# Clock-holding products, full-row broadcasts and a new order between the input projection and RWKV, in a two-layer hybrid SSD / RWKV-7 / mLSTM step on one Trainium2 core

## The chip, the cores and the metric

The kernel runs on one core of a Trainium2 chip. The metric is the device time of one execution in microseconds (us); lower is better. The engines are TensorE (PE; PEld is its weight load), VectorE (DVE), ScalarE (ACT), GpSimd (POOL) and SyncE (SP), which issues the transfers. The two levels of TensorE's clock that occur here are 1.2 and 2.4 GHz; the profile prints the granted clock as 0.50 and 1.00 (a stretch with both has a value between).

## The reference, cut to what matters

Two trunk layers work on 128 context tokens and 512 latent tokens, 640 in all, model width 1024. Float32 throughout.

```python
h = _rms_norm(x, norm1_g) * (1 + sc1) + sh1
u = h @ w_in                                   # one projection for three mixers
y_ssd  = ssd_mixer(...)      # Mamba-2, 8 heads of 64, chunks of 128, forward and backward, summed
y_rwkv = rwkv_mixer(...)     # RWKV-7, 4 heads of 64, forward and backward, summed
y_ml   = mlstm_mixer(...)    # 4 heads of 64, chunks of 128, forward and backward, summed
x = x + g1 * (concat(y_ssd, y_rwkv, y_ml) @ w_out)
x = x + g2 * ((silu(h2 @ ffn_w1) * (h2 @ ffn_w3)) @ ffn_w2)
```

In a chunk of the SSD scan, with t and s tokens of the chunk:

```python
decay  = exp(acum[t] - acum[s])  where s <= t, else 0
scores = einsum(C[t], B[s]) * decay
y      = einsum(scores, x * dt) + einsum(C[t], state_at_start) * exp(acum[t])
state' = state * exp(acum[last]) + einsum(exp(acum[last] - acum[s]), B, x * dt)
```

The mLSTM has the same form with its own gates (`wts`, `num`, `den`), and its output is `num / max(|den|, exp(-m))`. RWKV needs per token the decay, the rate `lr`, and the keys `kd = k * (1 + (lr - 1) * k_a)`; its two directions run as chunks of 128 with a small triangular inverse.

## The kernel before, in words

All 640 tokens stand as five chunks (NC = 5): chunk 0 is the context, 1 to 4 the latent tokens. Features lie on partitions, tokens along the free dimension. The body is written out for each of the two layers (`lay`), and each engine has its own hand-written program; semaphores (`s[...]`) tie them. The order of an engine's work is the order in which its program is written.

Of a layer, this is the part between the input projection and the RWKV scan, TensorE's side first:

1. After the last block of `w_in` (`mm3`, L878 to L880, three products of 320 columns for a float32-like result) come eight pairs of small products with the LoRA weights, 32 contraction rows each (L944, four rounds of four instructions). Each round waits until ACT has read the banks of the round before (`pair_read`, ACT at L1583).
2. The cached states are turned (L955, L959, L960), and the decays between chunks are spread over the partitions (L970, L972). ACT copies both out (L1674 to L1681). `token_major(c)` (L988 to L994) turns a chunk's features to tokens on partitions, ACT copies them (L1703 to L1707), DVE makes `XEB` from them (L2120, L2124) and POOL `VEB` (L685, `end_values`). `chunk_states(c)` (L1008 to L1031) multiplies these with the keys. TensorE runs `token_major(c + 1)` before `chunk_states(c)`.
3. The loop over chunks for y. `w_rows(c, i)`, i = 0 to 5, is a pair: one product that copies a row of log decays over all partitions (L1057; a selection column broadcast, 60 contraction rows, 512 columns) and one that adds the mask `NEG` of large negative numbers (L1058, bfloat16). ACT takes the exponential (L1719), four instructions a pair. `qk_products(c)` (L1113, L1117) gives the scores, DVE multiplies both (`weights`, L2143), and `y_ssd(c, g)` (L1089, and L1103 with the states for c > 0) and `y_mlstm(c)` (L1128, and L1140 with the states) use the result. `e_rows(c)` (L1072, 12 contraction rows) spreads the decays by which DVE scales the queries (`scaled_queries`). `mlstm_back(c)` (L1152) turns the mLSTM's result back after DVE's `normalise` (L2176 to L2184). Row products use banks 2, 3 and 5 in turn and wait until the bank has been read.
4. RWKV. POOL makes scaled keys (`chunk_keys`, L732 to L739), TensorE turns them (L1196, L1198) and makes diagonal blocks (L1207, L1212), DVE masks them (L2252 to L2263), then the inverse begins (L1221) and products with 256 columns follow (L1239).

DVE's side: `keys(c)`, in the loop of stage 2, works out what RWKV needs of its keys for all tokens (L2098, two instructions of 640 columns for c = 0 and 2; L2103 and L2104, 1280 columns each, for c = 1 and 3). POOL's side: after `end_values(c)` it scales the skip path of x (L688), then makes scaled values (`scaled_values`, L698) and combines states (`start_state`, L647 to L657); in RWKV it runs `chunk_keys(0)`, then `gates()` (L665 to L675, six passes over 640 to 2560 columns: the SSD gate and RWKV's bonus term), then `chunk_levels(k)` (L750) and `chunk_keys(k + 1)`. What `gates()` makes is read after the last RWKV chunk.

SELr has zeros in rows 60 to 127. RX is the left half of the buffer `whi`; its first 60 rows arrive by DMA.

## Time and profile before

| | |
|---|---|
| time, 3 runs | 2513.01 us median, 2505.12 to 2514.81 |
| the profiled execution | 2509.3 us, of which the span is 2507.6 us |
| busy, share of the span | PE 89%, PEld 82%, DVE 33%, ACT 30%, POOL 29% |
| mean granted clock of TensorE | 0.907 |
| chain that ended last, by engine | PE 80%, DVE 9%, ACT 4%, issue 3%, DMA 2%, POOL 2% |

The three projections' products (L878, L879, L880) hold 55% of the chain. They run at granted clock 1.00 for nearly all of their time. The part that the change touches stands between 292 and 480 us in layer 0 and between 1516 and 1700 us in layer 1. In the page's row of the granted clock, by fortieths of the span, these are the two places with the lowest digits (6, 5, 6 and 6, 5).

### The profile page before, as it was taken

How to read it: one execution, taken by the hardware profiler on the slowest of the kernel's cores; microseconds unless marked ns; L12 is line 12 of the kernel's file. 1: busy time of each engine (PE TensorE's matmuls, PEld its weight loads, DVE VectorE, ACT ScalarE, POOL GpSimd, SP SyncE). 2: the span in 40 equal slices, each digit the busy share in tenths (PEclk: the TensorE clock that was granted, in tenths of full speed). 3: DMA queues.
4: the chain of work that ended last, by engine and by line, in shares of the span. 5: the costliest groups of instructions: out<-in, count | busy, mean ns of one | idle time of the engine just before them, and what ended most of it. 6: DMA issues, size and time to landing. Idle time of an engine off the chain costs nothing.

```text
span 2507.6 us, 45740 instructions
## 1 busy us (share of the span) xinstructions
PE 2234.2 (89%) x20426; PEld 2044.9 (82%) x20426; DVE 821.7 (33%) x1363; ACT 762.1 (30%) x1348; POOL 723.0 (29%) x539
## 2 busy tenths in 40 slices
PE   5899899788797999999978998988887799999996
PEld 4899766677597999999878986657776799999986
DVE  4655153555512101010046453345544300101003
ACT  3435342232323222221153453323332422222111
POOL 4233150422022333332212322324221133333321
PEclk8999856799898999999989997659998999999998
DMA  6444200100021222243325431010001122222221
GB/s 222 136 142 126 58 7 1 35 5 3 1 60 51 76 76 76 76 123 114 85 82 156 142 105 19 1 34 5 3 2 33 42 78 73 73 75 74 70 61 57
DMA packets 260496, 166.66 MB, mean 66 GB/s; under 512 B 29938, under 2 KB 234228, under 8 KB 260300
## 3 DMA queue, kind: packets, MB, share of 16 engines
q1 hardware_dynamic: 259846, 163.59, 22.3%
q8 instruction: 161, 2.64, 0.4%
q14 instruction: 35, 0.29, 0.0%
q10 hardware_dynamic: 454, 0.14, 0.0%
HBM read 159.59 MB, written 4.12 MB: 65 GB/s over the span
## 4 chain that ended last, share of the span: by engine, by line
PE 80%; DVE 9%; ACT 4%; issue 3%; DMA 2%; POOL 2%; SPq 0%; DVEq 0%; ACTq 0%; POOLq 0%
PE PS L878 19%; PE PS L880 18%; PE PS L879 18%; PE PS L1221 4%; PE PS L829 2%; DMA ring<-in_w_in 2%; PE PS L1057 1%; PE PS L1089 1%; POOL ring_r L791 1%; PE PS L842 1%; PE PS L1058 1%; PE PS L1128 1%; DVE arena L1879 1%; PE PS L1103 1%; PE PS L1239 1%
## 5 line engine op out<-in xcount | busy, mean ns | idle before, releaser
L878 PE MATMUL PS<-rwp_r,whi_r 128*128 128x320 f32 x2880 | 912.6, 317 | 75.6 <-DVE arena_r L1883 35.9
L880 PE MATMUL PS<-rwp_r,ring_r 128*128 128x320 f32 x2880 | 901.4, 313 | 0.0
L791 POOL TENSOR_TENSOR ring_r<-ring,whi_r 128x1024 fp32r<-128x1024 f32 (+1 forms) x204 | 493.7, 2422 | 1254.4 <-ACT whi_r L1554 1254.4
L879 PE MATMUL PS<-arena_r,whi_r 128*128 128x320 f32 x2240 | 700.5, 313 | 0.0
L878 PEld LDWEIGHTS PS<-rwp_r,whi_r 128*128 128x128 f32 x2880 | 552.2, 192 | 93.4 <-issue 48.9
L880 PEld LDWEIGHTS PS<-rwp_r,ring_r 128*128 128x128 f32 x2880 | 551.4, 191 | 0.0
L879 PEld LDWEIGHTS PS<-arena_r,whi_r 128*128 128x128 f32 x2240 | 428.6, 191 | 0.0
L1554 ACT ACTIVATE whi_r<-ring 128x1024 fp32r<-128x1024 f32 (+1 forms) x204 | 211.5, 1039 | 678.6 <-PE PS L880 599.8
L879 PE MATMUL PS<-U_r,whi_r 128*128 128x320 f32 x960 | 300.3, 313 | 0.0
L2410 DVE TENSOR_TENSOR U<-arena,PS 128x640 f32<-128x640 f32 x44 | 36.1, 821 | 557.6 <-PE PS L880 557.6
L879 PEld LDWEIGHTS PS<-U_r,whi_r 128*128 128x128 f32 x960 | 183.8, 191 | 1.9 <-issue 0.2
L1221 PE MATMUL PS<-arena 64*64 64x64 f32 x3840 | 140.6, 226 | 49.1 <-DVE arena L2261 29.4
L2389 DVE SCALAR_TENSOR_TENSOR x<-PS,MOD,x 128x128 f32<-128x128 f32 (+2 forms) x96 | 36.1, 434 | 435.1 <-PE PS L880 435.1
L1221 PEld LDWEIGHTS PS<-arena 64*64 64x64 f32 x3840 | 127.7, 140 | 62.0 <-DVE arena L2261 32.3
L1820 ACT ACTIVATE arena<-PS 128x640 f32<-128x640 f32 x44 | 31.0, 705 | 271.5 <-PE PS L880 271.5
L1719 ACT ACTIVATE arena<-PS,arena 128x128 f32<-128x128 f32 x240 | 68.1, 373 | 129.5 <-PE PS L1058 125.4
L1751 ACT ACTIVATE arena<-PS 128x512 f32<-128x512 f32 (+1 forms) x100 | 55.5, 555 | 148.7 <-PE PS L1221 133.0
L1583 ACT ACTIVATE U<-PS 128x640 f32<-128x640 f32 x56 | 39.2, 699 | 152.8 <-PE PS L880 152.5
L1941 DVE SCALAR_TENSOR_TENSOR arena<-U,PC,arena 128x127 f32<-128x127 f32 x80 | 63.8, 817 | 51.9 <-ACT arena L1595 50.2
L750 POOL TENSOR_TENSOR arena<-arena,MKC 128x256 f32<-128x256 f32 x40 | 34.9, 893 | 138.6 <-DVE arena L2256 138.6
L829 PE MATMUL PS<-arena,ones 128*128 128x320 f32 x160 | 50.3, 450 | 22.4 <-ACT arena L1510 22.4
L732 POOL TENSOR_TENSOR arena<-rwp,U 128x256 f32<-128x256 f32 x20 | 14.6, 729 | 184.0 <-DVE U L2148 113.0
(364 smaller groups left out, 2793.9 us busy)
## 6 DMA issues: line engine op xcount, KB each, us to landing
ring<-in_ffn_w SPq DMA_DIRECT2D x120, 512.0 KB, 3.8
rwp<-in_ada_w SPq DMA_DIRECT2D x64, 512.0 KB, 4.1
ring<-in_w_in SPq DMA_DIRECT2D x50, 512.0 KB, 5.6
U<-in_ada_w SPq DMA_DIRECT2D x16, 512.0 KB, 10.1
ring<-in_w_out SPq DMA_DIRECT2D x16, 512.0 KB, 4.3
arena<-in_ada_w SPq DMA_DIRECT2D x16, 512.0 KB, 4.7
ring<-in_ffn_w SPq DMA_DIRECT2D x16, 384.0 KB, 3.4
out<-U SPq DMA_DIRECT2D x5, 512.0 KB, 2.7
```

The costliest lines, as they stand in the source:

```text
L791: g.tensor_tensor(rings_r[:, slot_of[n], 0:size(n), :], slot(n)[:, 0:size(n), :], whis[:, q_ % 2, 0:size(n), :].bitcast(F32), ALU.subtract ...
L829: ins = mm(PS[:, hf, 0:HALF], ones[:, :], tmp[:, k % 2, hf * HALF:(hf + 1) * HALF], start=k == 0, stop=k == KT - 1)
L878: mm(out, w[0][:, k, :], hi[:, cols], start=start, stop=False)
L879: mm(out, w[0][:, k, :], lo[:, cols], start=False, stop=False)
L880: return mm(out, w[1][:, k, :], hi[:, cols], start=False, stop=stop)
L1221: ins = mm(PS[t_, 4 * d + bank, col0 + 64 * hh:col0 + 64 * hh + 64], b[lhs][t_, hh, :], IDC[t_, :] if rhs is None else b[rhs][t_, hh, :], ...
L1554: A(whis[:, q % 2, 0:size(n), :], slot(n)[:, 0:size(n), :], ACT.Copy).then_inc(s["split_hi"], 1)
L1583: A(out.rearrange("p (a t) -> p a t", a=2), PS[:, b:b + 2, 0:HALF], func, **kw).then_inc(s["pair_read"], 1)
L1719: ins = A(W[:, i, q * P:(q + 1) * P], PS[:, ROW_BANK[(9 * c + i) % 3], q * P:(q + 1) * P], ACT.Exp, bias=COLS[:, c, 1, r + q:r + q + 1])
L1751: A(b["QQ"][:, w], PS[:, a + 2, :].rearrange("p (w h t) -> p w h t", w=2, h=4)[:, w], ACT.Copy).then_inc(s["inv_copy"], 1)
L1941: return v.scalar_tensor_tensor(out=out, in0=in_, scalar=s, in1=out, op0=ALU.mult, op1=ALU.add)
L2389: ins = v.scalar_tensor_tensor(out=xv[:, m, t0:t1], in0=PS[:, bank, c0:c0 + t1 - t0], scalar=g[:, cond:cond + 1], in1=xv[:, m, t0:t1], op0 ...
```

## The change

- A helper `warm(n, b)` issues n products of 128 rows and 512 columns (bfloat16 identity times `NEG`) into bank b. Nothing reads them. They stand: four ahead of the LoRA rounds and three behind each of the four rounds (bank 0), two ahead of each `chunk_states` wait (bank 4), eight ahead of the first wait for RWKV's keys and eight ahead of the first wait for its features (bank 7). That is 42 a layer.
- `w_rows` uses all 128 contraction rows instead of 60. `e_rows` becomes a pair: behind each of the three products one more of 128 rows adds a column of `NEG` that is all zero, 12 more products of 512 columns a layer.
- The turning of the states and the spreading of the decays move behind `token_major(0)`; ACT's copies of them move likewise (`states_in`). `qk_products(0)` moves ahead of the last `chunk_states`.
- In the loop, `mlstm_back(c - 1)` moves ahead of `y_ssd(c, 0)`; `y_mlstm` is cut in two, and the first three `w_rows` of the next chunk are spread around its second half and `qk_products`.
- DVE: `keys` has one instruction a chunk in stage 2; the three last passes move into the loop (`keys_end`, chunks 0 to 2, behind `weights`). POOL: the skip scaling leaves `end_values` and follows later; `gates()` moves from behind `chunk_keys(0)` to the end of RWKV.

```diff
@@ -702,11 +705,13 @@
                     def scans():
 ...
                         for c in range(NC):
                             end_values(c)
                         scaled_values(0)
+                        skip(0)
 ...
                         for k in range(1, 4):
                             start_state(k, 0)
+                        skip(1)
                         for c in range(2, NC):
                             scaled_values(c)
+                            skip(c)
@@ -754,11 +761,11 @@
                         chunk_keys(0)
-                        gates()
                         for k in range(NC):
                             chunk_levels(k)
                             if k < NC - 1:
                                 chunk_keys(k + 1)
+                        gates()
@@ -933,8 +940,15 @@
+                    def warm(n, b):
+
+                        for _ in range(n):
+                            mm(PS[:, b, :], identb[:, :], NEG[:, :].unsqueeze(1).broadcast_to((P, 2, 2 * P)),
+                               start=True, stop=True)
+
                     pe.wait_ge(s["lora_in"], at["lora_in"] + 48)
+                    warm(4, 0)
                     for i in range(0, len(LORAS), 2):
 ...
+                        warm(3, 0)
@@ -1001,6 +1019,7 @@
                         dirs = [d for d in range(2) if (c < 4 if d == 0 else c > 1)]
+                        warm(2, 4)
                         pe.wait_ge(s["xe_ready"], at["xe_ready"] + c + 1)
@@ -1033,10 +1052,25 @@
                     token_major(0)
+                    states_turned()
                     for c in range(NC):
                         if c < NC - 1:
                             token_major(c + 1)
+                        else:
+                            pe.wait_ge(s["ta_act"], at["ta_act"] + 4 * NC)
+                            qk_products(0)
                         chunk_states(c)
@@ -1054,7 +1088,7 @@
-                        mm(PS[:, b, :], SELr[0:NX, r:r + 1].broadcast_to((NX, P)), RX[0:NX, :], start=True, stop=False)
+                        mm(PS[:, b, :], SELr[:, r:r + 1].broadcast_to((P, P)), RX, start=True, stop=False)
@@ -1069,8 +1103,10 @@
-                            mm(PS[:, b, :], SELEr[e, i * P:(i + 1) * P], EX[e, :], start=True, stop=True).then_inc(
-                                s["ec_mm"], 1)
+
+                            mm(PS[:, b, :], SELEr[e, i * P:(i + 1) * P], EX[e, :], start=True, stop=False)
+                            mm(PS[:, b, :], identb[:, :], NEG[:, P - 1:P].broadcast_to((P, 4 * P)), start=False,
+                               stop=True).then_inc(s["ec_mm"], 1)
@@ -1153,27 +1183,28 @@
                         w_rows(c, 3)
+                        if c:
+                            mlstm_back(c - 1)
                         y_ssd(c, 0)
                         for i in range(4, 6):
                             w_rows(c, i)
                         y_ssd(c, 1)
-                        if c:
-                            mlstm_back(c - 1)
                         if c < NC - 1:
                             e_rows(c + 1)
                         y_mlstm(c)
                         if c < NC - 1:
+                            w_rows(c + 1, 0)
+                        y_mlstm_state(c)
+                        if c < NC - 1:
+                            w_rows(c + 1, 1)
                             qk_products(c + 1)
-                            for i in range(3):
-                                w_rows(c + 1, i)
+                            w_rows(c + 1, 2)
@@ -1185,6 +1216,8 @@
+                            if i == 0:
+                                warm(8, 7)
                             pe.wait_ge(s["rw_keys"], at["rw_keys"] + i + 1)
@@ -1200,6 +1233,8 @@
+                            if i == 0:
+                                warm(8, 7)
                             pe.wait_ge(s["rw_feat"], at["rw_feat"] + i + 1)
@@ -1705,8 +1743,10 @@
                         A(BKB[c % 2], PS[:, bk_, 0:384], ACT.Copy).then_inc(s["ta_act"], 1)
-                        if c > 0:
+                        if c:
                             chunk_states(c - 1)
+                        else:
+                            states_in()
@@ -2092,19 +2132,26 @@
-                        d = c // 2
-                        if c % 2 == 0:
-                            for f in range(2):
-                                ins = v.tensor_scalar(KD[d][:, f, :], BB[d][:, f, :], col(lay, "rwkv_k_a", f),
-                                                      KAO[:, f:f + 1], ALU.mult, ALU.add)
-                            ins.then_inc(s["dve_step"], 1)
+                        if c == 4:
+                            v.tensor_tensor(KD[0], KD[0], U[:, RK_:RK_ + 2, :], ALU.mult).then_inc(s["dve_step"], 1)
+                        else:
+                            d, f = c // 2, c % 2
+                            v.tensor_scalar(KD[d][:, f, :], BB[d][:, f, :], col(lay, "rwkv_k_a", f),
+                                            KAO[:, f:f + 1], ALU.mult, ALU.add).then_inc(s["dve_step"], 1)
+                        dve.wait_ge(s["dve_step"], step())
+
+                    def keys_end(c):
+
+                        if c == 0:
+                            v.tensor_tensor(KD[1], KD[1], U[:, RK_:RK_ + 2, :], ALU.mult).then_inc(s["dve_step"], 1)
+                        else:
+                            d = c - 1
+                            v.tensor_tensor(BB[d], BB[d], KK, ALU.mult).then_inc(
+                                s["rw_ready"] if d else s["dve_step"], 1)
 ...
@@ -2220,6 +2266,8 @@
                         for i in range(4, 6):
                             weights(c, i)
+                        if c < 3:
+                            keys_end(c)
                         y_back(c)
```

TensorE, from the LoRA rounds (L944, after: L958) to the states (L955, after: L976) and the first chunk (L988, after: L1006), before:

```order
L944 MATMUL PS<-arena,lora 128x320 x16
L955 MATMUL PS<-ident,arena 64x64 x8
...
L988 MATMUL PS<-ident,U 128x128 x4
L990 MATMUL PS<-ident,U 128x128 x2
L992 MATMUL PS<-ident,arena 128x24 x5
L994 MATMUL PS<-ident,U 128x128 x3
```

and now, where L946 is `warm`:

```order
L946 MATMUL PS<-NEG,identb 128x512 x4
L958 MATMUL PS<-arena,lora 128x320 x4
L946 MATMUL PS<-NEG,identb 128x512 x3
...
L1006 MATMUL PS<-ident,U 128x128 x4
L1008 MATMUL PS<-ident,U 128x128 x2
L1010 MATMUL PS<-ident,arena 128x24 x5
L1012 MATMUL PS<-ident,U 128x128 x3
L976 MATMUL PS<-ident,arena 64x64 x8
```

The first chunk's turning has passed the states, and unread products stand in each round.

TensorE, end of chunk 1 of the loop, before (L1072 is `e_rows`, L1128 and L1140 `y_mlstm`, L1113 and L1117 `qk_products`, L1057 and L1058 `w_rows`):

```order
L1152 MATMUL PS<-ident,arena 128x128 x4
L1072 MATMUL PS<-whi_r,SELE 128x512 x3
L1128 MATMUL PS<-ring,arena 128x65 x8
L1140 MATMUL PS<-arena 128x65 x8
L1113 MATMUL PS<-U 128x128 x2
L1117 MATMUL PS<-U 128x128 x4
L1057 MATMUL PS<-whi_r,SEL 128x512
L1058 MATMUL PS<-NEG,identb 128x512
```

and at the end of chunk 0 now (same roles: L1107 and L1108, L1153, L1058 and L1062, L1091 and L1092; chunk 0 has no part with states, in the others it stands between the first two pairs of L1091):

```order
L1107 MATMUL PS<-whi_r,SELE 128x512
L1108 MATMUL PS<-NEG,identb 128x512
L1153 MATMUL PS<-ring,arena 128x65 x8
L1091 MATMUL PS<-whi_r,SEL 128x512
L1092 MATMUL PS<-NEG,identb 128x512
...
L1058 MATMUL PS<-U 128x128 x2
L1062 MATMUL PS<-U 128x128 x4
...
L1182 MATMUL PS<-ident,arena 128x128 x4
L1125 MATMUL PS<-arena,whi 64x128 x8
```

Products of 512 columns now stand on both sides of each narrow part, and the turning back (L1182) has moved behind them.

POOL at the start of RWKV, before:

```order
L739 TENSOR_TENSOR arena<-U 128x2x128
L665 TENSOR_TENSOR U<-U 128x2560
L670 TENSOR_TENSOR U<-rwp 128x1280
L672 TENSOR_TENSOR U<-U 128x1280
L675 TENSOR_SCALAR U<-U,PC 128x640 x2
L750 TENSOR_TENSOR arena<-arena,MKC 128x256 x4
```

and now:

```order
L746 TENSOR_TENSOR arena<-U 128x2x128
L757 TENSOR_TENSOR arena<-arena,MKC 128x256 x4
```

The four lines of `gates()` are gone from here; they stand behind the fifth L757.

## Rows read from the trace of the kernel before

**Rows 1.** Windows view: stretch, us, busy PE, PEld, DVE, ACT, POOL, clock, DMA.

```profile
292.93:308.28 15.35, 8.85 (x32) 4.56 (x33) 0.08 (x1) 7.07 (x9) 0.00 (x0) 0.58 0.20 34
308.28:346.04 37.76, 33.20 (x257) 27.39 (x258) 22.66 (x23) 13.46 (x44) 18.56 (x17) 0.59 0.10 12
346.04:457.07 111.03, 104.72 (x596) 71.00 (x594) 41.40 (x83) 36.84 (x129) 22.18 (x33) 0.61 0.00 1
457.07:476.96 19.89, 8.84 (x140) 7.65 (x140) 13.17 (x12) 2.34 (x5) 19.10 (x12) 0.50 0.40 106
1516.61:1530.92 14.31, 7.85 (x32) 4.07 (x33) 0.08 (x1) 7.07 (x9) 0.00 (x0) 0.64 0.22 37
1530.92:1566.90 35.98, 31.16 (x259) 25.80 (x259) 22.66 (x23) 13.54 (x44) 18.26 (x17) 0.64 0.08 12
1566.90:1678.97 112.07, 106.44 (x596) 71.14 (x594) 41.41 (x83) 37.10 (x129) 22.09 (x33) 0.59 0.00 1
```

**Rows 2.** The same columns, two slices of the loop over chunks.

```profile
370.00:372.50 2.50, 2.50 (x18) 1.73 (x16) 0.00 (x0) 0.00 (x0) 0.00 (x0) 0.50 0.00 0
397.50:400.00 2.50, 2.50 (x33) 2.04 (x29) 0.00 (x0) 0.88 (x4) 0.95 (x1) 1.00 0.00 0
```

**Rows 3.** Timeline, TensorE, at granted clock 0.50: start us, us, engine, line, operation.

```profile
356.39 1.65 PE L1072 MATMUL PS<-whi_r,SELE 12*128 12x512 f32 x3
357.96 3.68 PE L1128 MATMUL PS<-ring,arena 128*128 128x65 f32 x16
...
362.16 1.06 PE L1117 MATMUL PS<-U 64*128 64x128 f32 x8
...
372.97 0.79 PE L1057 MATMUL PS<-whi_r,SEL 60*128 60x512 f32 x1
...
374.23 1.98 PE L1089 MATMUL PS<-arena,whi 128*64 128x128 f32 x16
```

**Rows 4.** Timeline, TensorE, at granted clock 1.00.

```profile
396.09 0.50 PE L1057 MATMUL PS<-whi_r,SEL 60*128 60x512 f32 x1
...
396.52 0.39 PE L1058 MATMUL PS<-NEG,identb 128*128 128x512 bf16 x1
...
396.84 1.09 PE L1089 MATMUL PS<-arena 128*64 128x128 f32 x16
...
449.49 2.00 PE L1128 MATMUL PS<-ring,arena 128*128 128x65 f32 x16 [1.71 <-DVE arena L2143]
...
451.42 1.77 PE L1140 MATMUL PS<-arena,lora 64*128 64x65 f32 x16
```

**Rows 5.** Timeline, TensorE: three waits outside the loop (in brackets, us and releaser).

```profile
295.90 2.50 PE L944 MATMUL PS<-arena,lora 32*128 32x320 f32 x8 [1.62 <-ACT rwp L1583]
...
343.32 1.12 PE L1025 MATMUL PS<-arena 128*64 128x256 f32 x4 [4.02 <-DVE arena L2124]
...
459.16 1.08 PE L1196 MATMUL PS<-ident,arena 128*128 128x128 f32 x4 [2.10 <-POOL arena L733]
```

**Rows 6.** Waits, 308.28 to 477 us: who waited for whom, total us, times, longest.

```profile
PE PS L1128 <- DVE arena L2143: 3.4, 3, 1.7
```

**Rows 7.** Groups by line, DVE, 292.93 to 476.96 us: busy us, mean ns.

```profile
L2261 DVE TENSOR_TENSOR arena<-arena,MKC 128x256 f32<-128x256 f32 x2 | 6.0, 3002 | 0.1
...
L2263 DVE TENSOR_TENSOR arena<-arena,MKC 128x256 f32<-128x256 f32 x2 | 3.5, 1760 | 0.0
```

**Rows 8.** Timeline, POOL and DVE, RWKV's chunk 0 (463 us) and chunk 4 (619 us).

```profile
463.09 5.59 POOL L665 TENSOR_TENSOR U<-U 128x2560 f32<-128x2560 f32 x1
...
474.82 4.05 POOL L675 TENSOR_SCALAR U<-U,PC 128x640 f32<-128x640 f32 x2
...
619.32 0.43 DVE L2261 TENSOR_TENSOR arena<-arena,MKC 128x256 f32<-128x256 f32 x1
...
619.66 0.95 DVE L2263 TENSOR_TENSOR arena<-arena,MKC 128x256 f32<-128x256 f32 x1
...
648.96 4.70 POOL L791 TENSOR_TENSOR ring_r<-ring,whi_r 128x1024 fp32r<-128x1024 f32 x2 [25.77 <-ACT whi_r L1554]
```

More of the change, by code:

```diff
@@ L1034, in chunk_states, with qk_products @@
                         ins.then_inc(s["cs_mm"], 1)
+                    def qk_products(c):
+                        for q in range(2):
+                            mm(PS[:, q, 0:P], U[64 * q:64 * q + 64, BT_, ck(c)],
+                               U[64 * q:64 * q + 64, CT_, ck(c)], start=True, stop=True)
+                        for hh in range(ML_H):
+                            f, q = hh // 2, hh % 2
+                            ins = mm(PS[:, q, (1 + f) * P:(2 + f) * P], U[64 * q:64 * q + 64, MK + f, ck(c)],
+                                     U[64 * q:64 * q + 64, MQ + f, ck(c)], start=True, stop=True)
+                        ins.then_inc(s["qk_mm"], 1)
                     token_major(0)
+                    states_turned()
                     for c in range(NC):
```

100 lines of the change are left out of this document (46 added, 54 removed).

## The prediction, as it was put on record

> **What bounds the kernel now.** Read the page's chain first: TensorE holds 80% of it, and the big projections run at granted clock 1.00, so nothing there is open to this change. Then read the row of the granted clock by fortieths: its two lowest places are the stretch between `w_in` and RWKV, once a layer. Then cut that stretch into its four stages with the windows view [rows 1]. Layer 0: LoRA rounds 15.35 us, states and tokens 37.76, the loop over chunks 111.03, the start of RWKV 19.89, together 184.0; layer 1 has 182.3 (its fourth stage is the same to 0.01 us). In the loop TensorE is busy for 104.72 of 111.03 us, at a mean clock of 0.61, while DVE has 41 us and ACT 37. So the loop is bound by TensorE, and mostly by TensorE at the lower of its levels, 1.2 GHz. What matters is how the same products look at both levels. At 0.50 a `w_rows` pair takes 1.26 us (start of L1057 to start of what follows, 372.97 to 374.23), sixteen L1089 records 1.98, sixteen L1128 records 3.68 [rows 3]. At 1.00 these are 0.75 (396.09 to 396.84), 1.09 and 2.00 [rows 4]. Apart from the pair the ratio is 1.82 to 1.84; with start-to-start times it is a little more, and I take 1.86 (pair: 1.68). The loop, all of it at 1.00, would be a third shorter.
>
> What moves the clock? Being busy alone does not raise it here: TensorE was busy 2.50 of 2.50 us in a slice at 0.50 and in another at 1.00 [rows 2]. The slices differ in what streams: long moving operands and full rows in one, short ones with 60, 64 or 12 rows in the other. A wait does lower it: the LoRA rounds have 32 rows and waits of 1.62 us [rows 5], and their mean is 0.58 and 0.64 [rows 1].
>
> **The change part by part**, layer 0 first, each stage first with the clock held at 1.00.
>
> *LoRA rounds.* Four rounds, each a product group and ACT's reading of it. 2.50 us at 0.50 makes 1.35 at 1.00; with the wait of 1.62 [rows 5] a round takes 2.97. Three of these, the last group, and three unread products on the path (the nearest row is L1058, the same operands: 0.32 from its start to that of the next at 1.00 [rows 4], less where nothing has to be loaded or waited for between them; I take 0.25) give 8.9 + 1.35 + 0.75 = 11.0. The other unread products lie in the waits: three are 0.75 to 1.0 us in 1.62. They are covered as long as ACT's reading is what the round waits for, and it stays so. 15.35 becomes 11.2, a gain of 4.1; layer 1, 14.31, gains 3.1.
>
> *States and tokens.* PE busy 33.20 at mean clock 0.59 means a low share of 0.82: 27.2 us low and 6.0 high [rows 1]. At 1.00 that is 14.6 + 6.0 = 20.6. The wait of 4.02 for DVE's XEB [rows 5] goes, because DVE does one key pass a chunk instead of up to two long ones and POOL's skip scaling no longer stands beside it. New: `token_major(1)` now waits for ACT's seven copies of the states, which before ran ahead of everything (13.46 us for 44 ACT instructions is 0.31 each, 2.1 us); ten unread products, 2.5 us, since at 1.00 these find few waits; and 2 to 3 us because DVE's and POOL's steps for one chunk, 3 us or so (22.66 us of DVE over five chunks, less the passes moved), are now nearly as long as TensorE's 4. Together 28: gain 9.8; layer 1, 35.98, gains 8.0.
>
> *Loop.* One chunk at 1.00: six pairs 4.5; turning back no more than L1089's 1.1; the y products four times 1.02, 4.1; `e_rows`, now three pairs, 2.25; L1128 1.95; L1140 1.77 [rows 4]; `qk_products` 0.9 (eight of its twelve records take 1.06 at 0.50 [rows 3], so 1.6 at most low). Sum 16.5. Chunk 0 up to its L1128 is set by ACT and DVE rather than TensorE, and I leave it 10 us. Then four chunks, without the last `e_rows`: 4 x 16.5 - 2.25 = 63.8; the last L1128, L1140, normalising and turning back 6.3. That is 80, with 2 for waits 82. The gain is 29.0, and from 112.07 in layer 1 30.1. A second way to the same: 104.72 busy at 0.61 is 81.7 low and 23.0 high, 66.9 at 1.00, plus `e_rows` 12 x 0.43 = 5.2, plus the idle 6.3: 78.4.
>
> The move of `mlstm_back(c - 1)` costs nothing: DVE's result is there 1.5 us behind L1140, and three pairs and `qk_products` lie between. The early `w_rows(c + 1, 0)` waits for DVE to have read an `e_rows` bank; `keys_end` stands ahead of that on DVE with 1.5 to 2.3 us. L1128 hides it; if DVE ran later than I think this would be the next wait (2 us a chunk for three chunks, 6 a layer at most). DVE with 41 us in 111 has room. POOL's skip scalings stand behind the states they could delay or ahead by one instruction; each has a chunk's slack.
>
> *Start of RWKV.* Three gains and a cost. POOL's `gates()` runs from 463.09 to 478.87 [rows 8]; beside it DVE's L2261 and L2263 take 6.0 and 3.5 us for two each [rows 7], in chunk 4, with POOL not at it, 0.43 and 0.95 apiece [rows 8]. So 9.5 - 2.8 = 6.7 us go, whatever the clock does. At the end of RWKV the gates need 15.8 us of POOL, which idles 25.77 there [rows 8]; DVE's work there reads PSUM, so I cost it at nothing, and at up to 5 us if that cover fails. TensorE's 8.84 us at 0.50 become 4.75 at 1.00: 4.1 less. Of the sixteen unread products the first eight about fit the wait of 2.10 [rows 5] at 1.00 (2.0, up to 2.5); the other eight stand where nothing is waited for and put 2.0 on the path, too. Net 6.7 + 4.1 - 2.0 = 8.8, say 9.0 with what the first products behind the stage save.
>
> *Row counts.* Widening L1057 from 60 to 128 rows adds no time: 512 columns stream either way, and the 12-row L1072 with three such products takes 1.65 us [rows 3], no less for each than the 128-row ones. The Trainium skill says the same (TensorE: Matmul & The Clock Gate, the table under "Why this matters for your kernels": a product over 32 rows takes as long as one over 128).
>
> Sum with the clock held: layer 0 4.1 + 9.8 + 29.0 + 9.0 = 51.9, layer 1 3.1 + 8.0 + 30.1 + 9.0 = 50.2, together 102.
>
> **How far the clock holds.** This is the whole question, and no row answers it. For: every drop in the loop before falls into L1072, L1128 and the wait behind them, and there now stand full-row pairs on both sides. Against: L1128 and L1140 stay what they are, 16 records of 65 columns in 2 us, and behind the states' small products TensorE still waits for ACT. I take half a chunk a layer at 0.50 in the loop (a chunk would take 29 instead of 16.5 us, so 6) and one turning and one set of states in stage 2 (3). That is 9 a layer: 102 - 18 = 84, and 2509.3 - 84 = 2425. This is on the scale of the profiled execution, 3.7 us under the median of 2513.0, which is well within the spread shown.
>
> **The rivals.**
> *A, held throughout:* 2509.3 - 102 = 2407. For it: the change puts something into each place where the clock fell. Chance 0.28.
> *B, only waits count, not rows or widths.* Then the filled waits hold the clock in stages 1, 2 and 4, but the loop, 94% busy already, stays at 0.61: it pays for `e_rows` (12 x 0.74 low, 0.43 high: 8) and gains its waits (3.4 [rows 6] and 1): +4. Layer 0: -4.1 - 6.8 - 8 + 4 = -15; layer 1 -12. Time 2482. For it: stage 1's drop. Against it: the full slice at 0.50 [rows 2]. Chance 0.10. The Trainium skill (same page, same table) asks only that TensorE be kept busy without gaps; by that the loop should have been at 1.00 all along, and the trace disagrees.
> *C, half the loop's gain:* the clock falls at every L1128 and rises some 5 us later. The loop gains 10 to 14 instead of 23: 2509.3 - 2 x 31 = 2447. Chance 0.15.
> *D, slower.* The clock falls at the same places, and all that was added runs at 0.50. Per layer: `e_rows` 12 x 0.74 = 8.9, ten unread products at up to 0.61 in stage 2 6.1, sixteen at the start of RWKV less the 2.10 wait 7.7, three behind LoRA 1.8: 24.5. Against it stand 6.7 (gates), 4.0 (DVE wait), 4.4 (loop waits) and 1.6 (LoRA's last wait): 16.7. So +8 a layer, 2525. It decides when the loop gains less than 8 us a layer from the clock. Chance 0.04.
> *E, no effect* because something outside, such as the DMA of the next weights, sets the pace: DMA's share in the four stages is 0.40 at most [rows 1] and `w_out` is requested only behind the loop. Chance 0.01.
>
> **How the numbers follow.** Forecast 0.42 (2410 to 2440), A 0.28, C 0.15, B 0.10, D 0.04, E 0.01. The range from 2402 (A, with 5 for a chunk 0 that is shorter than I gave it) to 2462 (C with the upper wait costs) holds about 0.82. A measurement of this kernel can tell some 0.5%, 12.5 us. A, the forecast, C and B are faster than 2500.5 (0.95, less a little for an error common to all: 0.93), E and the edge of B the same (0.03), D slower (0.04).
>
> **What would show it.** The four stages in the windows view: 11, 31, 88 and 11 us, clock above 0.9 in the first, third and fourth. L1128's sixteen records near 2.0 us in most chunks; the two L2261 of chunk 0 at 0.43 each; POOL's gates inside the last RWKV chunk with no wait of ACT for them. The step most likely to be wrong is the clock between `e_rows` and `qk_products`: if L1128 still shows 3.7, B or D is true. A wait of TensorE for `w_rows` on DVE's scaling would show that `keys_end` came at the wrong place.

## The result, and the profile after

| | before | after |
|---|---|---|
| median, 4 runs each | 2509.07 us (2498.75 to 2514.81) | 2405.51 us (2389.97 to 2408.29) |
| profiled execution, span | 2509.3, 2507.6 us | 2408.3, 2406.6 us |
| mean granted clock of TensorE | 0.907 | 0.950 |

The ratio is 0.9579, 95% interval 0.9525 to 0.9633: 4.2% faster. Forecast were 2425 us in a range of 2402 to 2462. The measured time lies inside it, but 20 us under the forecast and within 2 us of rival A (2407). Two executions of the experiments' kernels below stood far off the others (2546.37 us with 64 rows, 6430.74 us with 128 rows alone); the medians count them, the ratios don't.

The windows view of after, the same four stages of both layers (LoRA, states and tokens, loop, start of RWKV; columns as in [rows 1]):

```profile
292.49:303.37 10.88, 8.24 (x46) 3.98 (x46) 0.04 (x1) 6.14 (x8) 0.13 (x1) 1.00 0.29 48
303.37:333.94 30.57, 28.69 (x269) 22.44 (x268) 14.60 (x20) 13.81 (x46) 11.24 (x11) 0.78 0.12 14
333.94:411.24 77.30, 72.93 (x604) 51.96 (x604) 46.52 (x86) 36.24 (x129) 31.25 (x39) 0.90 0.01 1
411.24:424.09 12.85, 9.42 (x156) 6.38 (x157) 5.79 (x12) 2.34 (x5) 9.21 (x12) 0.90 0.64 164
1462.05:1475.84 13.79, 11.79 (x45) 5.22 (x45) 0.04 (x1) 6.74 (x9) 0.13 (x1) 0.70 0.24 38
1475.84:1508.15 32.31, 30.82 (x270) 24.25 (x268) 14.61 (x20) 13.22 (x45) 11.25 (x11) 0.71 0.09 14
1508.15:1585.47 77.32, 73.00 (x604) 52.03 (x604) 46.49 (x86) 36.23 (x129) 31.25 (x39) 0.90 0.00 1
1585.47:1598.36 12.89, 9.44 (x156) 6.42 (x157) 5.79 (x12) 2.34 (x5) 9.22 (x12) 0.90 0.60 165
```

| us | LoRA | states, tokens | loop | start of RWKV | sum |
|---|---|---|---|---|---|
| before, layers 0 and 1 | 15.4, 14.3 | 37.8, 36.0 | 111.0, 112.1 | 19.9, 19.9 | 366.3 |
| forecast for after | 11 | 31 | 88 | 11 | 282 |
| after | 10.9, 13.8 | 30.6, 32.3 | 77.3, 77.3 | 12.9, 12.9 | 267.9 |

The four stages give 98 of the 101 us by which the span fell: the change acts where it stands and nearly nowhere else. Two thirds of it (69 us) come from the loop over chunks. That stage, the largest, is the one that was forecast worst: it is 10.7 us shorter in each layer than it should have been, while the start of RWKV is 1.9 longer.

One turn of the loop, from one `y_mlstm` (L1153) to the next, in layer 0 of after:

```profile
343.36:357.00 13.64, 13.37 (x119) 9.35 (x118) 10.38 (x18) 6.48 (x24) 12.54 (x18) 1.00 0.01 2
357.00:371.56 14.56, 14.49 (x135) 10.33 (x134) 9.64 (x16) 6.65 (x24) 7.76 (x8) 1.00 0.00 1
371.56:390.70 19.14, 19.07 (x135) 13.62 (x134) 10.12 (x19) 6.64 (x24) 2.31 (x2) 0.73 0.00 1
390.70:403.66 12.96, 12.41 (x130) 9.39 (x128) 6.50 (x14) 6.64 (x24) 0.00 (x0) 1.00 0.01 3
```

So the clock was not held throughout: one turn has it at half speed for about ten of its 19 us, which costs 4.6 us against the turn before with the same products. But a whole turn at full clock takes 14.56 us where the prediction had 16.5 (the turns of 13.64 and 12.96 us lack the part with states and the `e_rows`). The question for the experiments is what made it shorter, and which edit brought the clock.

### The profile page after: what moved, and what is told of

Read it like the earlier page. It is cut to its first block, busy times and chain, and to the rows that moved or that the text cites. A ratio compares the mean times of both kernels' runs of the same rounds, so it can differ in the third digit from the quotient of the medians.

```text
span 2406.6 us, 45954 instructions
## 1 busy us (share of the span) xinstructions
PE 2168.1 (90%) x20534; PEld 1996.4 (83%) x20534; DVE 801.7 (33%) x1363; ACT 759.3 (32%) x1348; POOL 728.8 (30%) x539
## 4 chain that ended last, share of the span: by engine, by line
PE 80%; DVE 8%; ACT 5%; issue 3%; DMA 3%; POOL 2%; SPq 0%; DVEq 0%; ACTq 0%
PE PS L885 19%; PE PS L886 19%; PE PS L887 19%; PE PS L1256 5%; DMA ring<-in_w_in 2%; PE PS L836 2%; PE PS L849 1%; POOL ring_r L798 1%; DVE arena L1919 1%; PE PS L1274 1%; DVE arena L1911 1%; PE PS L1401 1%; PE PS L1091 1%; PE PS L1322 1%; ACT whi_r L1589 1%
## 5 line engine op out<-in xcount | busy, mean ns | idle before, releaser
L798 POOL TENSOR_TENSOR ring_r<-ring,whi_r 128x1024 fp32r<-128x1024 f32 (+1 forms) x204 | 494.5, 2425 | 1217.1 <-ACT whi_r L1589 1217.1
L1256 PEld LDWEIGHTS PS<-arena 64*64 64x64 f32 x3840 | 127.1, 140 | 49.9 <-DVE arena L2309 19.9
L757 POOL TENSOR_TENSOR arena<-arena,MKC 128x256 f32<-128x256 f32 x40 | 36.6, 935 | 147.9 <-DVE arena L2304 147.9
L2321 DVE TENSOR_TENSOR arena<-arena,PS 128x256 f32<-128x256 f32 x100 | 40.4, 419 | 73.0 <-PE PS L1256 72.8
```

The source lines that it names most:

```text
L798: g.tensor_tensor(rings_r[:, slot_of[n], 0:size(n), :], slot(n)[:, 0:size(n), :], whis[:, q_ % 2, 0:size(n), :].bitcast(F32), ALU.subtract ...
L1256: ins = mm(PS[t_, 4 * d + bank, col0 + 64 * hh:col0 + 64 * hh + 64], b[lhs][t_, hh, :], IDC[t_, :] if rhs is None else b[rhs][t_, hh, :], ...
L2321: v.tensor_tensor(b["X"], b["X"], heads(PS[:, 4 * d + 3, 0:256], 4), ALU.add).then_inc(s["inv_add"], 1)
```

## The experiments

All medians stand against runs of the kernel before on the same chip (2509 to 2518 us in the various groups), so the ratios are what is compared. "Us" behind a ratio is that ratio applied to 2510. The loop's columns are from one profiled execution of each kernel.

| kernel | ratio, 95% interval | us gained | loop, layers 0 and 1: us (clock) |
|---|---|---|---|
| after | 0.9579 (0.9525 to 0.9633) | 106 | 77.3 (0.90), 77.3 (0.90) |
| after again | 0.9556 (0.9501 to 0.9611) | 111 | 77.3 (0.90), 77.3 (0.90) |
| after, 60 rows | 0.9626 (0.9589 to 0.9663) | 94 | 97.8 (0.73), 78.3 (0.94) |
| after, 64 rows | 0.9672 (0.9632 to 0.9713) | 82 | 97.8 (0.73), 85.9 (0.84) |
| after, 96 rows | one run, 2397.95 us | 111 | 72.8 (0.97), 77.4 (0.90) |
| after, no unread products | 0.9557 (0.9506 to 0.9608) | 111 | 73.0 (0.98), 78.6 (0.88) |
| after, no zero column | 0.9617 (0.9585 to 0.9649) | 96 | 80.5 (0.83), 81.6 (0.84) |
| after, old order in the loop | 0.9610 (0.9575 to 0.9645) | 98 | 81.4 (0.94), 81.3 (0.94) |
| after, no zero column, none unread in RWKV | 0.9600 (0.9565 to 0.9635) | 100 | 79.5 (0.85), 81.6 (0.84) |
| before, 128 rows alone | 0.9767 (0.9719 to 0.9814) | 58 | 88.7 (0.77), 83.4 (0.89) |
| before, unread products and zero column alone | 0.9836 (0.9798 to 0.9873) | 41 | 99.4 (0.74), 81.6 (0.96) |
| before, gates later alone | 0.9895 (0.9856 to 0.9933) | 26 | 109.2 (0.61), 109.2 (0.61) |
| before, 128 rows with gates later | 0.9733 (0.9704 to 0.9762) | 67 | 83.3 (0.89), 88.3 (0.79) |

(The gain with 96 rows is its one run against the 2509.26 of before in its group.)

### Row counts of the broadcasts

Seen first in the trace of after, against the prediction's "adds no time". The timeline of TensorE in after at full clock, two pairs in a row (L1091 broadcasts, L1092 adds the mask; the first column is the start):

```profile
395.89 0.50 PE L1091 MATMUL PS<-whi_r,SEL 128*128 128x512 f32 x1
396.23 0.39 PE L1092 MATMUL PS<-NEG,identb 128*128 128x512 bf16 x1
396.27 0.58 PE L1091 MATMUL PS<-whi_r,SEL 128*128 128x512 f32 x1
396.69 0.39 PE L1092 MATMUL PS<-NEG,identb 128*128 128x512 bf16 x1
396.92 1.05 PE L1182 MATMUL PS<-ident,arena 128*128 128x128 f32 x8
```

The second broadcast begins 0.04 us behind the start of the mask product, since its weights are loaded meanwhile (PEld, same stretch):

```profile
396.23 0.10 PEld L1092 LDWEIGHTS PS<-NEG,identb 128*128 128x128 bf16 x1 [0.15 <-issue]
396.23 0.20 PEld L1091 LDWEIGHTS PS<-whi_r,SEL 128*128 128x128 f32 x1
```

First run: after with the one line put back.

```diff
-mm(PS[:, b, :], SELr[:, r:r + 1].broadcast_to((P, P)), RX, start=True, stop=False)
+mm(PS[:, b, :], SELr[0:NX, r:r + 1].broadcast_to((NX, P)), RX[0:NX, :], start=True, stop=False)
```

> The kernel after, with the row broadcasts back at 60 contraction rows. In the trace of after two such pairs behind one another start 0.46 us apart at the full clock, before it was 0.75. Theory L (loading): weights of 128 rows are loaded while the product before still runs, weights of 60 rows are not. Then pairs are at 0.74 again at the full clock, the loop's clock stays as in after, and 30 pairs x 0.2 x 2 layers give about +13: 2418 on after's 2406. Theory K (clock): the rows hold the clock. Then the loop falls to the low level in most chunks, sixteen L1153 take 3.2 to 3.7 us, the loop is over 95 us instead of 77 and the time is 2440 or more. Both can be true; the pair's spacing at the full clock tells L, the granted clock of the loop tells K.

Measured: 2423.63 us, 0.9626. The same two pairs stand 0.73 us apart in it at full clock (398.33, 399.06), where after has 0.38, so theory L holds. Its loops in the windows view:

```profile
337.60:435.41 97.81, 92.85 (x600) 63.37 (x604) 46.52 (x86) 36.73 (x129) 31.38 (x39) 0.73 0.00 1
...
1528.94:1607.27 78.33, 73.58 (x600) 50.26 (x604) 46.33 (x86) 36.29 (x129) 31.41 (x39) 0.94 0.00 1
```

Layer 0 came out as theory K had it (over 95 us, clock 0.73), layer 1 did not (78.3 us at 0.94), and the time lies between the two theories' times. So a loop with 60 rows can still run near full clock when the other edits are in. The intervals of the whole (0.9589 to 0.9663 here, 0.9525 to 0.9633 for after) overlap, so by the time alone the rows' worth on top of the rest, some 12 us, isn't shown. The reverse, the kernel before with 128 rows and nothing else:

> The kernel before with nothing but the row broadcasts over 128 rows. Theory L: the pair at the low clock goes from 1.26 to 0.9 or less and at the full clock from 0.75 to 0.46 to 0.55; 30 pairs a layer give 8 to 11 us a layer, 2485 to 2492 from 2509 without any gain in clock. Theory K alone: pairs stay at 1.26 and 0.75, but the mean clock of the loop rises from 0.61 to 0.7 or more, worth 10 to 20 us a layer. Both: 2450 to 2470. Neither (only the new order holds the clock): 2509.

Measured: 2463.82 us, 0.9767, so 58 of the change's some 108 us from one line, as "both" had it (2450 to 2470). Its loops in the windows view:

```profile
344.69:433.36 88.67, 79.71 (x594) 57.31 (x592) 41.36 (x83) 34.73 (x129) 21.84 (x33) 0.77 0.00 1
...
1545.95:1629.39 83.44, 71.05 (x594) 51.02 (x592) 41.18 (x83) 34.75 (x129) 21.84 (x33) 0.89 0.00 1
```

These are 22 and 29 us shorter than before's, with the clock at 0.77 and 0.89 in place of 0.61 and 0.59. Even at half clock a pair in the series gets shorter: 0.88 us (395.71 to 396.59), where [rows 3] had 1.26. Which row counts do this? After with 64 rows, then with 96:

```diff
+mm(PS[:, b, :], SELr[0:64, r:r + 1].broadcast_to((64, P)), RX[0:64, :], start=True, stop=False)
```

> The kernel after, with the row broadcasts over 64 contraction rows instead of 128 (rows 60 to 63 of the stationary tile are zero; nothing that is computed changes). Theory 1 (only all 128 rows let a pair's weights be loaded behind the product before): pairs stay 0.74 us start to start at full clock as with 60 rows, and the whole is 2420 to 2425 us. Theory 2 (it needs a row count that fills 64, and 60 misses that): pairs at 0.46 us, the whole within 3 us of after.

> The kernel after with the row broadcasts over 96 contraction rows instead of 128. If only the full 128 rows let the weights be loaded behind the running product: pairs 0.74 us start to start at full clock, 2420 to 2432 us in all. If any count over 64 does: pairs at 0.46 us and 2400 to 2412 us.

Measured: 2432.4 us (0.9672) with 64, more than either theory had; one run of 2397.95 with 96. In the timeline of the kernel with 64 rows the pairs are 0.72 us apart, and the load of the second begins only when the mask product is through (398.67 and its 0.32):

```profile
398.27 0.47 PE L1091 MATMUL PS<-whi_r,SEL 64*128 64x512 f32 x1
398.67 0.39 PE L1092 MATMUL PS<-NEG,identb 128*128 128x512 bf16 x1
398.99 0.50 PE L1091 MATMUL PS<-whi_r,SEL 64*128 64x512 f32 x1
```

```profile
398.99 0.18 PEld L1091 LDWEIGHTS PS<-whi_r,SEL 64*128 64x128 f32 x1 [0.23 <-ACT arena L1759]
```

With 96 rows the pairs are as with 128; the loop of layer 1 is, too (77.4 us), that of layer 0 is 4.5 us shorter at a higher clock (timeline of TensorE, then the windows view of layer 0's loop):

```profile
395.38 0.49 PE L1091 MATMUL PS<-whi_r,SEL 96*128 96x512 f32 x1
395.72 0.39 PE L1092 MATMUL PS<-NEG,identb 128*128 128x512 bf16 x1
395.76 0.58 PE L1091 MATMUL PS<-whi_r,SEL 96*128 96x512 f32 x1
```

```profile
333.84:406.68 72.84, 67.94 (x604) 48.27 (x604) 46.51 (x86) 36.14 (x129) 31.20 (x39) 0.97 0.01 1
```

So of the row broadcasts, whose weights are 128 columns wide, those for 96 or 128 rows are loaded while the product over 128 rows before them runs, those for 12, 60 or 64 only after it. "Only all 128 rows" was wrong, and so was "any count that fills 64". The row count isn't all that matters: L1125's weights have 128 rows, but 64 columns, and are loaded 0.32 us behind the mask product's, too (PEld, the kernel with 96 rows):

```profile
396.18 0.10 PEld L1092 LDWEIGHTS PS<-NEG,identb 128*128 128x128 bf16 x1 [0.25 <-issue]
396.50 0.85 PEld L1125 LDWEIGHTS PS<-arena 128*64 128x64 f32 x16 [0.23 <-issue]
```

A full pair between narrow products gains less (0.64 us for 0.75). Over the six pairs of a chunk at full clock, start to next start, after has 0.64 + 0.66 + 0.38 + 0.65 + 0.38 + 0.74 = 3.45 us and the kernel with 60 rows 0.75 + 0.73 + 0.73 + 0.66 + 0.74 + 0.75 = 4.36. That is 0.9 us a chunk, under 5 us a layer; at half clock 1.26 becomes 0.69 to 1.18. In the kernel before and the one with 128 rows alone, the thirty pairs of a loop add up to 35.3 and 36.7 us against 24.5 and 24.0 (start to next start, each counted with 1.3 us at most, so that long waits stay out). So 11 and 13 of the 22 and 29 us lie in the pairs, the clock's share in them included. The rest is in the other products, which have the same operands in both kernels and differ by the clock.

### The unread products

After, with `warm` issuing nothing:

```diff
-                        for _ in range(n):
+                        for _ in range(0):
                             mm(PS[:, b, :], identb[:, :], NEG[:, :].unsqueeze(1).broadcast_to((P, 2, 2 * P)),
```

> The kernel after, without the 42 products a layer that nothing reads (those of the two or three stages around the loop; the zero column in the decay rows stays). Theory 1: they hold the clock in the LoRA rounds only; the rounds go from 10.9 to about 15 us, stage 2 is low for as long as now or longer (+0 to +4 a layer), the start of RWKV saves the products on its path (2 to 4 us) and loses them again at the low level. Sum +5 to +10 a layer, 2416 to 2428. Theory 2: the loop depends on entering it at the full clock; then the loop too falls, and the time is over 2440.

Measured: 2407.83 us, 0.9557, no different from after. The expectation was missed: the LoRA rounds take 13.66 us in both layers, no longer than three of after's four (13.8), the start of RWKV is 1.1 us shorter, and the loops keep a clock of 0.98 and 0.88. The kernel before with these alone (and the zero column):

> The kernel before with the unread products alone (in the LoRA stage, ahead of the chunk states' wait, at the start of RWKV) and the zero-column products in the decay rows; broadcasts over 60 rows, orders, keys and gates as before. Theory 1 (they lift the clock where they stand): LoRA falls from 15 towards 11 us, the loop's mean clock rises from 0.6 towards 0.75 and the loop falls by 10 us or more a layer; 2475 to 2490 us. Theory 2 (without the 128-row broadcasts there is no gain, since the loop's clock follows from those): loop 108 to 112 us, whole 2500 to 2515 us.

Measured: 2467.73 us, 0.9836: 41 us, and the time is 7 us under theory 1's range. Its loops, still with 60 rows, have

```profile
339.55:438.90 99.35, 93.65 (x608) 62.05 (x606) 41.45 (x83) 35.91 (x129) 22.09 (x33) 0.74 0.00 1
...
1548.08:1629.68 81.60, 74.13 (x607) 49.73 (x604) 41.36 (x83) 35.52 (x129) 22.61 (x34) 0.96 0.00 1
```

against 0.61 and 0.59 of before. They are 42 us shorter together, the six other stages only 4.5. Of what this kernel adds, only the zero column stands in the loop; the unread products stand ahead of it and behind it. So the 41 us are not shown to be theirs: the column may have brought most of it, and the run above, without unread products and with the column, speaks for that. The kernel before with the column alone was not run, and the split stays open. What is shown is that a set without full-row broadcasts lifts the loop's clock, too, and that the unread products add nothing to the rest of the change. The first loop also shows that the same program comes out at 0.74 in one layer and at 0.96 in the other.

The zero column is in the loop itself, so it was taken out of after by itself (12 products a layer; the text on record says nine, which is wrong):

```diff
-mm(PS[:, b, :], SELEr[e, i * P:(i + 1) * P], EX[e, :], start=True, stop=False)
-mm(PS[:, b, :], identb[:, :], NEG[:, P - 1:P].broadcast_to((P, 4 * P)), start=False,
-   stop=True).then_inc(s["ec_mm"], 1)
+mm(PS[:, b, :], SELEr[e, i * P:(i + 1) * P], EX[e, :], start=True, stop=True).then_inc(s["ec_mm"], 1)
```

> The kernel after, without the product of the zero column that follows each of the nine decay-row products a layer (the sum it closed is the same without it). Theory 1 (its time is what it takes of TensorE): nine products of 512 columns a layer at about 0.22 us each at full clock are 2 us a layer, 4 in all; 2401 us. Theory 2 (it fills TensorE's waits and keeps the clock): the loop's mean granted clock falls from 0.90 towards the 0.6 of the kernel before and the loop grows by 5 us or more a layer; 2415 us or more. Theory 3 (it stands in waits and the clock doesn't need it): within 2 us of after.

Measured: 2413.9 us, 0.9617. The whole differs from after by less than the intervals; the stages say more. `e_rows` itself takes 0.89 us in place of 2.13, since twelve-row products behind each other stand 0.30 apart, yet the loop is longer (timeline, then windows, both layers):

```profile
395.70 0.95 PE L1107 MATMUL PS<-whi_r,SELE 12*128 12x512 f32 x3
396.59 2.00 PE L1152 MATMUL PS<-ring,arena 128*128 128x65 f32 x16
```

```profile
336.75:417.22 80.47, 73.71 (x592) 53.29 (x592) 46.60 (x86) 36.19 (x129) 31.27 (x39) 0.83 0.01 1
...
1512.20:1593.84 81.64, 74.01 (x592) 53.09 (x592) 46.85 (x86) 36.18 (x129) 31.20 (x39) 0.84 0.00 1
```

Five us of products are gone and the loop has grown by 3.2 and 4.3, at a clock of 0.83 and 0.84. The four loops without the column (these two and those of the next kernel) have 0.83 to 0.85; the eight with it in kernels that are otherwise like after in the loop (after twice, 96 rows, no unread products) 0.88 to 0.98. That is theory 2's mechanism at a smaller size than it gave (a clock towards 0.6, 5 us a layer, 2415 us or more). The two groups don't overlap, but their nearest loops, 78.6 and 79.5 us, are only 0.9 us apart.

The same with the sixteen products at the start of RWKV taken out, too:

> The kernel after, without the sixteen unread products a layer at the start of RWKV and without the zero-column products in the decay rows. Theory 1 (both cost what their columns take): RWKV's start is 1.1 us a layer shorter, as in the kernel without any unread product, and the loop up to 2 us a layer; 2399 to 2403 us. Theory 2 (they keep the clock for what follows): the start of RWKV falls back to half clock, its stage stays at 12.9 us or grows; 2406 us or more.

Measured: 2411.64 us, 0.9600. Neither theory is right by itself: the loop is that of the kernel without the column, as it should be, and the start of RWKV (layer 0) falls to half clock, as theory 2 had it, and is still no longer, 12.58 us for 12.85:

```profile
415.03:427.61 12.58, 8.86 (x142) 7.66 (x141) 6.38 (x12) 2.34 (x5) 9.17 (x12) 0.50 0.65 168
```

### The order

Only TensorE's order inside a chunk back to the old one, all else as after:

```diff
-                        if c:
-                            mlstm_back(c - 1)
                         y_ssd(c, 0)
 ...
                         y_ssd(c, 1)
+                        if c:
+                            mlstm_back(c - 1)
 ...
                             qk_products(c + 1)
-                            w_rows(c + 1, 2)
+                            for i in range(3):
+                                w_rows(c + 1, i)
```

> The kernel after, with TensorE's order inside a chunk as in the kernel before: the two mLSTM back-transposes of the chunk before behind the second SSD product, and the first three row broadcasts of the next chunk behind the mLSTM state part and the q-k products. Theory 1 (the new order fills waits, as the prediction's loop term has it): VectorE's and ScalarE's readers get their rows later, each chunk is 1 to 2 us longer, 8 to 16 us in all; 2413 to 2421 us. Theory 2 (the loop's gain is the rows and the clock alone): within 3 us of after, 2402 to 2409.

Measured: 2412.65 us, 0.9610; loops 81.4 and 81.3, 4 us longer than after's, as theory 1 had it. Its waits view, TensorE, the loop of layer 0 (engine, who waited for whom, us in total, times, longest):

```profile
PE PS L1125 <- DVE arena L2187: 5.1, 5, 1.0
PE PS L1091 <- ACT arena L1757: 2.0, 5, 0.7
PE PS L1153 <- DVE arena L2187: 1.7, 1, 1.7
```

The same of after:

```profile
PE PS L1125 <- DVE arena L2189: 1.0, 1, 1.0
PE PS L1091 <- ACT arena L1759: 0.7, 1, 0.7
PE PS L1153 <- DVE arena L2189: 0.5, 1, 0.5
```

The old order leaves TensorE 11.5 us idle in the loop (81.35 less 69.83 busy), the new one 4.4. The busy time at the old order is less, because its clock is 0.94, so the clock is not what the new order brings: it brings the waits for VectorE's `weights` behind other work. The intervals of the whole overlap with after's; the length of the loop is the same to 0.1 us in all four loops of after's two traces, and to 0.1 us in both of this one.

### The gates

The kernel before with `gates()` behind RWKV's last chunk:

> The kernel before with only POOL's gates moved to the end of RWKV. Theory: DVE's two L2261 and L2263 in RWKV's chunk 0 fall from 9.5 to 2.8 us, POOL's 15.8 us fit into its idle time at the end: -6.7 a layer, 2496. Rival: DVE or ACT pays in the last chunk for what was saved in the first; then no more than 3 us a layer.

Measured: 2491.87 us, 0.9895. Start of RWKV 12.6 and 11.8 us for 19.9, 7.3 and 8.1 less; the loop is 2 to 3 us shorter, too, and the cause of that is open. The stage in layer 0, where VectorE is busy 5.79 us in place of 13.17:

```profile
454.90:467.50 12.60, 8.84 (x141) 7.65 (x141) 5.79 (x12) 2.34 (x5) 9.21 (x12) 0.50 0.63 168
```

Then the two edits together, before with 128 rows and with this (the text on record speaks of the keys of chunk 0 as well; the edit moves only `gates()`):

> The kernel before with the two edits that gained alone: the row broadcasts over 128 rows, and the RWKV keys of chunk 0 and the gates later. Theory 1 (the gains add): 2463.8 alone and 2491.9 alone against 2517.9 and 2509 to 2518 of before give 45 to 54 and 17 to 26 us, together 2440 to 2450 us; what then lacks to 2405.5 is that of the new order and of the unread products. Theory 2 (they share the clock's gain): 2452 us or more.

Measured: 2441.93 us, 0.9733: 67 us (60 to 74), inside theory 1's 2440 to 2450, while the gains of the two alone by their ratios add up to 84 with some 10 us of uncertainty on each. So they add, or overlap by a little; the intervals don't settle it. The spans of the profiled executions speak for adding: 49.7 and 17.4 us alone, 64.3 together. What lacks to after (39 us or more) is not that of the unread products, which are worth nothing on top. It is left for the order, the key passes moved out of stage 2 and the zero column; the key passes were not run by themselves. That kernel has 38.1 us in stage 2, after without unread products 31.7 and 34.5.

### After a second time

> The kernel after, unchanged, a second time, for a second trace and a median beside these runs. If its loop's clock is a matter of chance, its stages differ from the first trace (loop 77.3 and 77.3 us, clock 0.90 and 0.90) by several us, and the differences of 3 to 4 us a layer of the kernels without the zero column and with the old order mean little; if they are 77 to 78 us again, those differences stand. Whole: 2400 to 2410 us.

Measured: 2404.1 us, 0.9556. The loops again:

```profile
336.57:413.89 77.32, 73.07 (x604) 52.17 (x604) 46.52 (x86) 36.24 (x129) 31.26 (x39) 0.90 0.01 1
...
1514.11:1591.42 77.31, 73.00 (x604) 52.03 (x604) 46.52 (x86) 36.25 (x129) 31.27 (x39) 0.90 0.00 1
```

So the differences of 3 to 4 us a layer stand against after's own loops. They are not far from the scatter of close relatives, though: with the same loop, the kernels with 96 rows and without unread products have 72.8 to 78.6 us. And the four executions of this kernel run from 2382.25 to 2417.81 us, at a mean clock of 0.962 to 0.945, so the clock falls differently in executions that have no trace. LoRA of layer 0 doesn't repeat: 13.79 us at clock 0.69 here, 10.88 at 1.00 above, with the same instructions.

No kernel of these is measurably faster than after. `e_rows` over 96 or 128 rows, which by the pairs might gain once more, was not tried.

## Why the prediction was right, and where not

**Bound and direction: right.** The stretch was bound by TensorE at its lower level, and the clock rose from 0.6 to 0.90 in the loop. Rival B (only waits count) is out: 128 rows alone fill no wait and raise the loop's clock to 0.77 and 0.89 from 0.61 and 0.59. D is out with it, and the fall of stage 4 by gates alone was as large as put (6.7 forecast, 7.3 and 8.1 measured).

**LoRA: right in layer 0, wrong in layer 1.** A round is 3.00 us from start to start (292.49 to 295.49), 2.97 forecast, with the wait that was expected:

```profile
295.49 1.35 PE L958 MATMUL PS<-arena,lora 32*128 32x320 f32 x8 [0.90 <-ACT rwp L1618]
```

But the unread products don't hold the clock there with certainty: three of the four LoRA stages in the two traces of after are at 0.69 or 0.70 and 13.8 us long, no shorter than without any unread product (13.66 at 0.58). The forecast's layer 1, 11.2 us, was 2.6 too low.

**States and tokens: right in size**, 30.6 and 32.3 us for 31, though at a clock of 0.78 and 0.71 in place of nearly 1.00 less 3 us. That is luck in part: two errors cancel. TensorE is idle 1.9 us of the stage in layer 0 and 1.5 in layer 1, where the sum had 2.1 for ACT's copies and 2 to 3 for the longer steps of VectorE and GpSimd; and the clock, low for some 40 to 60% of the time, cost more than the 3 us put for it.

**The loop: the term that was mis-sized.** Two sizes in it failed. One is "Widening L1057 from 60 to 128 rows adds no time", which was taken to mean no change either way: of the 16.5 us for a chunk the six pairs were 4.5; at full clock they are 3.45, of which the rows give 0.9 (4.36 with 60). The other is the price of the narrow products, which the prediction takes from the last chunk alone [rows 4]: L1140's 1.77 is 1.32 in the others (L1170, 359.35 to 360.67), L1128's 1.95 is 1.70 (L1153, 357.00 to 358.70). With 0.3 from the rest this makes 14.56, the turn from 357.00 to 371.56 above. Four of these less the last `e_rows` are 56 instead of 63.8 us: 8 of the 10.7, and over half of these 8 from the pairs. The remaining 3 lie in the allowances: 2 us for waits between the chunks, of which hardly any are there, and 0.6 for chunk 0 (9.42 us for 10). The allowance for the clock was good: half a chunk at the low level, 6 us a layer. One turn shows it,

```profile
371.56 3.26 PE L1153 MATMUL PS<-ring,arena 128*128 128x65 f32 x16
```

at 4.6 us more than its neighbour, and one more low piece stands at the loop's end (7.58 us behind the last turn at a clock of 0.65, forecast 6.3). So 2405.5 is near rival A's 2407 by luck, without A being true: the clock did fall, and cheaper pairs and narrow products made up for it. The rule that I cited from the Trainium skill (TensorE: Matmul & The Clock Gate, the table under "Why this matters for your kernels", 32 rows as long as 128) holds for the products themselves here, 0.49 us at 12 rows and 0.50 at 128. The duration isn't what the forecast lacked: it lacked what the next product's load can overlap with, and that the runs above show.

**Start of RWKV: 12.9 for 11.** Gates were right, and their cover at the end, too: GpSimd still idles 10.40 us behind them (they are five passes, not the six that the text ahead of the prediction has).

```profile
597.53 4.69 POOL L798 TENSOR_TENSOR ring_r<-ring,whi_r 128x1024 fp32r<-128x1024 f32 x2 [10.40 <-ACT whi_r L1589]
```

What failed is "TensorE's 8.84 us at 0.50 become 4.75 at 1.00: 4.1 less". The work did get as short (9.42 us busy, 4.3 of it unread products), but the stage didn't: gates alone brought it to 12.60 at clock 0.50, and after has 12.85 at 0.90. TensorE's products there stand between waits for others, so most of what a faster one saves is waited away:

```profile
416.71 1.89 PE L946 MATMUL PS<-NEG,identb 128*128 128x512 bf16 x8
...
420.57 1.15 PE L1256 MATMUL PS<-arena 64*64 64x64 f32 x32 [0.87 <-DVE arena L2309]
422.56 1.60 PE L1256 MATMUL PS<-arena 64*64 64x64 f32 x32 [0.84 <-DVE arena L2309]
```

GpSimd's records show what is left. From its first pass for scaled keys (L739; eight of them take 5.5 us) to its last masking (L757), in after and in the kernel without unread products:

```profile
411.78 0.73 POOL L739 TENSOR_TENSOR arena<-rwp,U 128x256 f32<-128x256 f32 x1 [37.91 <-DVE U L2194]
...
422.12 1.83 POOL L757 TENSOR_TENSOR arena<-arena,MKC 128x256 f32<-128x256 f32 x2 [0.16 <-DVE arena L2304]
```

```profile
410.98 0.72 POOL L739 TENSOR_TENSOR arena<-rwp,U 128x256 f32<-128x256 f32 x1 [32.48 <-DVE U L2194]
...
420.68 1.83 POOL L757 TENSOR_TENSOR arena<-arena,MKC 128x256 f32<-128x256 f32 x2 [0.16 <-DVE arena L2304]
```

That is 10.34 us with the sixteen products and 9.70 without (9.70 also in the kernel that lacks only these and the column, at half clock). So the sixteen cost 0.6 us a layer net, where the sum had 2.0 for the eight on the path. The clock counts only for what follows: from that last L757 to the stage's end it is 1.5 us at full clock and 2.3 at half. So a full clock is worth up to 0.8 us here and not 4.1, and with the sixteen products gone the stage took 11.7 to 11.8 us where the clock had risen by its end and 12.5 to 12.6 where it hadn't.

**The order and VectorE's slack: right.** The wait of `w_rows` for VectorE, allowed for at 2 us a chunk, is 0.3 us once in the waits view, and nothing in TensorE's waits is put down to the moved key passes (L2149).

**Still open** is what decides where the clock falls. The same loop had 0.90 in four records, 0.97 or 0.98 in one layer of two close relatives and 0.74 in one layer of another with 0.96 in its second; a low stretch of about ten us costs 4.6, and the steps between are of about that size. Being busy doesn't settle it: in the kernel before with unread products and zero column TensorE was busy for 15.00 of 15.00 us (395 to 410) at a granted clock of 0.50 throughout. And since the edits change the pairs' length, the rows and the neighbours of each product at once, which of these the clock answers to is not shown.

## What to carry to other kernels

Where short products over few contraction rows alternate with full ones, look at the start-to-start times and at the weight load, not at the product's duration: widening a broadcast from 60 or 64 rows to 96 or more, with zeros in the selection, let the load run beside the product before and was the cheapest edit here (58 us from one line, most of it with the clock's help). Means that lift the same clock are worth less together than alone (the full rows 58 us alone and some 12 on top of the rest): measure each alone and each taken out of the whole. The unread products were worth nothing on top of the rest; alone they were only measured together with the zero column. Take a stage's own waits before pricing a faster clock in it; where it waits for another engine, only what stands behind the last wait gets shorter (0.8 us of 12.6 here).

## What the runs showed of the hardware that was not expected

- Behind a product over 128 rows, weights of 128 columns for 12, 60 and 64 rows were loaded only once it had ended (pairs 0.72 to 0.75 us apart at full clock, 1.26 at half with 60), for 96 and 128 rows beside it (0.38; at half clock 0.69 to 0.88 with 128). Weights of 128 rows and 64 columns (L1125) were not loaded beside it either. Twelve-row products behind twelve-row ones stand 0.30 apart.
- Adding twelve full-row products a layer whose result changes nothing went with a loop that is 3 to 4 us shorter (77.3 us for 80.5 and 81.6).
- The granted clock of the same instructions differed between layers and executions of one kernel (LoRA 1.00 or 0.70, 10.9 or 13.8 us), while the loop's length repeated to 0.1 us in after's two traces.
- TensorE busy 15.00 of 15.00 us stood at a granted clock of 0.50 (395 to 410 in the kernel before with unread products and zero column).
